# Attention weights and values: one fp32 product in place of three split products

## What is computed

```python
z = einsum('bhtd,bhsd->bhts', qb, kb) * scale
causal = s_idx < t_idx
log_beta = log_sigmoid(z)
log_skip_j = where(causal, log_sigmoid(-z), 0.0)
log_skip = cumsum(log_skip_j, axis=3, reverse=True) - log_skip_j
weights = where(causal, exp(log_beta + log_skip), 0.0)
outs.append(einsum('bhts,bhsd->bhtd', weights, vb))
```

## Time and profile before

| | |
|---|---|
| median of three runs | 1186.79 us |
| the profiled execution | 1186.26 us |
| its span, first to last instruction | 1184.4 us |
| PE (TensorE matmul) busy | 1171.7 us, 99% of the span |
| DVE (VectorE) busy | 783.7 us, 66% |
| ACT (ScalarE) busy | 419.6 us, 35% |
| POOL (GpSimd) busy | 148.8 us, 13% |
| mean granted TensorE clock | 0.997 |

### The profile page before, as it was taken

One profiled execution on the slowest core, in us unless ns is written; L12 is line 12 of the kernel. 1 busy time (PEld: TensorE's weight loads), 2 busy tenths in 40 slices (PEclk: granted clock), 3 DMA queues, 4 the chain that ended last, 5 costly groups with the idle time before them and its releaser, 6 DMA issues. The chain is left out here.

```text
span 1184.4 us, 20326 instructions
## 1 busy us (share of the span) xinstructions
PE 1171.7 (99%) x7268; PEld 1078.3 (91%) x7268; DVE 783.7 (66%) x1576; ACT 419.6 (35%) x911; POOL 148.8 (13%) x344
## 2 busy tenths in 40 slices
PE   8999999999999999999999999999999999999998
PEld 7999999999999999887888989898999999999787
DVE  5657485766767675673544777778787878788521
ACT  4545353545445453552222222323232222222200
POOL 2322121213031311110003100000000000000000
PEclk8999999999999999999999999999999999999999
DMA  8220223223132301065632110314141421117431
GB/s 241 62 54 19 72 81 103 77 82 102 70 115 72 108 1 46 10 243 197 200 107 72 54 36 19 116 64 145 61 142 65 139 75 52 46 36 282 158 138 71
DMA packets 110657, 113.49 MB, mean 96 GB/s; under 512 B 6880, under 2 KB 86752, under 8 KB 110560
## 3 DMA queue, kind: packets, MB, share of 16 engines
q1 hardware_dynamic: 110560, 112.23, 29.6%
HBM read 79.70 MB, written 32.51 MB: 95 GB/s over the span
## 5 line engine op out<-in xcount | busy, mean ns | idle before, releaser
L28 PE MATMUL p_proj<-w_qkv_hi,ut_hi 128*128 128x384 f32 x512 | 176.1, 344 | 2.5 <-DVE ut_lo L792 2.5
L30 PE MATMUL p_proj<-w_qkv_hi,ut_lo 128*128 128x384 f32 x512 | 173.0, 338 | 0.0
L29 PE MATMUL p_proj<-w_qkv_lo,ut_hi 128*128 128x384 f32 x512 | 172.5, 337 | 0.0
L28 PE MATMUL p_proj<-w_ig_hi,next_hi 128*128 128x256 f32 x512 | 145.7, 284 | 0.0
L29 PE MATMUL p_proj<-w_ig_lo,next_hi 128*128 128x256 f32 x512 | 143.1, 280 | 0.0
L30 PE MATMUL p_proj<-w_ig_hi,next_lo 128*128 128x256 f32 x512 | 143.1, 280 | 0.0
L28 PE MATMUL p_proj<-next_hi,w_qf_hi 128*128 128x512 f32 x282 | 113.3, 402 | 0.0
L30 PE MATMUL p_proj<-next_hi,w_qf_lo 128*128 128x512 f32 x282 | 110.2, 391 | 0.0
L29 PE MATMUL p_proj<-next_lo,w_qf_hi 128*128 128x512 f32 x282 | 109.9, 390 | 0.0
L804 DVE TENSOR_TENSOR_SCAN a_skip<-a_skip,a_diagonal 128x129 f32<-128x129 f32 (+3 forms) x64 | 86.9, 1358 | 31.5 <-ACT a_beta L648 29.6
L28 PEld LDWEIGHTS p_proj<-w_qkv_hi,ut_hi 128*128 128x128 f32 x512 | 97.1, 190 | 3.9 <-DVE w_qkv_lo L772 2.4
(11 more groups left out here) (238 smaller groups left out, 2751.2 us busy)
## 6 DMA issues: line engine op xcount, KB each, us to landing
stage<-in_hg_w_in_dram SPq DMA_DIRECT2D x32, 512.0 KB, 4.6
stage<-in_sb_w_in_dram SPq DMA_DIRECT2D x29, 512.0 KB, 5.8
w_out_hi_scratch<-m_in SPq DMA_DIRECT2D x32, 256.0 KB, 2.1
w_out_lo_scratch<-m_in SPq DMA_DIRECT2D x32, 256.0 KB, 2.3
m_in<-mixed_scratch SPq DMA_DIRECT2D x12, 448.0 KB, 5.8
a_beta<-in_x_dram SPq DMA_DIRECT2D x8, 512.0 KB, 4.4
m_in<-in_sb_w_out_dram SPq DMA_DIRECT2D x16, 256.0 KB, 3.8
ut_hi<-w_out_hi_scratch SPq DMA_DIRECT2D x8, 512.0 KB, 8.5
```

The lines of the kernel that those rows point to most:

```text
L28: pe.matmul(out, w_hi, m_hi, start=start, stop=False, skip_group_check=True)
L29: pe.matmul(out, w_hi, m_lo, start=False, stop=False, skip_group_check=True)
L30: return pe.matmul(out, w_lo, m_hi, start=False, stop=stop, skip_group_check=True)
```

## The change

Values are kept in one fp32 tile `v`, written by one copy of VectorE. Weights are kept in one fp32 tile `wt`, written by ScalarE's copy, which now raises `wt_ready` itself. VectorE's `split_weights` is gone, and with it the semaphores `wt_hi_ready` and `v_hi_ready`. `outputs` makes one fp32 product per block. The tables, the projections, the scores and all of layer 1 are as before.

```diff
-        v_hi = [sb(f"v_hi{b}", [P, TILES, P], F32R) for b in range(2)]
-        v_lo = [sb(f"v_lo{b}", [P, TILES, P], F32R) for b in range(2)]
+        v = [sb(f"v{b}", [P, TILES, P]) for b in range(2)]
...
-        wt_hi = sb("wt_hi", [P, TILES, 2, P], F32R)
-        wt_lo = sb("wt_lo", [P, TILES, 2, P], F32R)
+        wt = sb("wt", [P, TILES, 2, P])
...
-                act.activation(wt_hi[:, blocks, j % 2, :],
-                               bank[:, 0:blocks.stop - blocks.start, :], ACT.Copy).then_inc(wt_hi_ready, 1)
+                act.activation(wt[:, blocks, j % 2, :],
+                               bank[:, 0:blocks.stop - blocks.start, :], ACT.Copy).then_inc(wt_ready, 1)
...
-            def split_weights(h, j, u, bank):
-
-                dve.wait_ge(wt_hi_ready, UNITS * h + ENDS[j] - Z_UNITS[j] + u + 1)
-                if not (known_first(h) and j < 2):
-                    dve.wait_ge(o_done, PAIRS * h + j // 2)
-                blocks = unit_blocks(j, u)
-                dve.tensor_tensor(wt_lo[:, blocks, j % 2, :], bank[:, 0:blocks.stop - blocks.start, :],
-                                  wt_hi[:, blocks, j % 2, :].bitcast(F32),
-                                  ALU.subtract).then_inc(wt_ready, 1)
...
-                        dve.tensor_copy(v_hi[nb][:, t, :], raw[t % 4][:, 2, :]).then_inc(v_hi_ready, 1)
-                        dve.wait_ge(v_hi_ready, NAT * n + t + 1)
-                        dve.tensor_tensor(v_lo[nb][:, t, :], raw[t % 4][:, 2, :], v_hi[nb][:, t, :].bitcast(F32),
-                                          ALU.subtract).then_inc(v_ready, 1)
+                        dve.tensor_copy(v[nb][:, t, :], raw[t % 4][:, 2, :]).then_inc(v_ready, 1)
...
-                    w_h = wt_hi[:, s, :, :] if s <= 2 * g else wt_hi[:, s, 1, :]
-                    w_l = wt_lo[:, s, :, :] if s <= 2 * g else wt_lo[:, s, 1, :]
-                    last = matmul_exact(pe, o, v_hi[b][:, s, :], v_lo[b][:, s, :], w_h, w_l,
-                                        s == 0, s == 2 * g + 1)
+                    last = pe.matmul(o, v[b][:, s, :], wt[:, s, :, :] if s <= 2 * g else wt[:, s, 1, :],
+                                     start=s == 0, stop=s == 2 * g + 1, skip_group_check=True)
```

More of the change, by code:

```diff
@@ L425, in build_attention @@
         raw_ready = sem("raw_ready")
-        v_hi_ready = sem("v_hi_ready")
         v_ready = sem("v_ready")
@@ L441, in build_attention @@
         weights_turned = sem("weights_turned")
-        wt_hi_ready = sem("wt_hi_ready")
         wt_ready = sem("wt_ready")
@@ L821, in attend @@
                         last_head_lo(half, tile)
[L822 to L825, removed]
             def last_head_lo(b, part):
```

## The result

The changed kernel takes 1192.17 us (median of five runs, 1191.01 to 1192.68) against 1187.15 us before (1186.08 to 1187.77, five runs). The ratio is 1.0042, with a 95% interval of 1.0031 to 1.0052: slower by 5.0 us, where 8.0 us was forecast. The profiled execution took 1192.68 us, the slowest of the five. TensorE's granted clock was 1.00, the 2.4 GHz level, from 17 us to the end of the products in both profiled executions, so their rows may be compared directly.

What follows compares the result with a forecast made beforehand. TensorE's streaming was taken to bound the kernel (99% busy): +10.5 us of streaming less 2.5 of stalls gives +8.0, from 1186.26 to 1194.3 us for the profiled execution, 1194.8 for the median; range 1190.5 to 1198.5.

Steps and rivals of the forecast that it cites:

- Two instructions, two passes: In outputs, one fp32 product is two instructions, each streaming its columns twice; likeliest case, 0.88 with its whole range.
- The price of 0.45 us: Cost of one 256-column fp32 product in outputs, 0.43 to 0.46 us, against 0.352 split; streaming +10.5 us in all.
- the cheap end: Low end of the likeliest case: 0.43 us a product and 4.2 us of stalls gone, +3.7, 1190.5 us; no own chance.
- The stalls: TensorE's waits at three places for the weights' lower part: 2.5 us given back, at least 1.2, at most 4.2.
- the first stall: TensorE's wait around 497.25 us, before outputs: 1.4 us, of which 0.9 comes back and 0.5 stays, for ScalarE's copy.
- the second: TensorE's wait before the outputs at 529.97 us, behind VectorE's scan and product: 1.15 us, all of it to go.
- third: TensorE's last wait for the lower part, after the product ending at 537.72 us: 0.45 us, all to go.
- What costs nothing: VectorE's lost work, ScalarE's copy and later `o_done` and `o_gated` add no time; layer 1 lasts as long as before.
- The bound of 3 us: If cover failed at the last eight groups of outputs (0.7 us): under 3 us, 1 us kept in the range.
- One pass: Rival: every fp32 instruction streams once, 0.235 us per 256-column product in outputs, 1167.3 us in all; chance 0.08.
- Three passes: Rival: an fp32 product's two instructions stream three times together, 0.35 us, level with split; chance 0.04, including level results.
- The level rival: Three passes in outputs: only 2.1 us of 128-column gain and 2.5 of stalls left, 1182.3 us; chance 0.04, including level results.

Runs made afterwards that it cites:

- The experiment that takes the waits alone: Changed kernel with F32R tiles and three products per block, all of upper parts, lower parts left out (doesn't compute the reference): 1184.82 us, ratio 0.999.
- The two kernels run side by side: "Streaming only" again, 1194.59 us (ratio 1.0068), and the same with the second VectorE operation on each value tile put back, 1193.07 us (ratio 1.0053).
- Streaming only: Changed kernel with VectorE's subtraction of the weights put back, into a tile that nothing reads, and raising `wt_ready`: 1194.1 us, ratio 1.0063.

## Why the prediction was right

The sign and the mechanism held: TensorE's stream sets the time, one fp32 product is two instructions that each take up about the time of twice their columns, and VectorE's relief is worth only the stalls. The size was 8.0 us where 5.0 was measured. The account of the 5.0 is: +8.0 of streaming, -1.3 at the other products of the attention, -2.5 of stalls, +0.8 in layer 1. Step by step:

- **Two instructions, two passes.** Right. The trace after has 320 instructions for 160 products, 0.216 us apart at 256 columns and 379 ns long (390 was forecast), and halving the width changes little. The decisive rows were the durations of the earlier trace rows; the steps of 0.11 us would have been the same either way. The reading of the earlier trace rows worked with a slightly smaller step than it names (0.06 us for 128 columns gives 191 and 176 ns, not 193 and 178), and 195 fits 64 columns all the same. What the runs can't tell apart is an instruction that makes two passes and one that streams once at half the rate: the time is the same. The rule of the Trainium skill that a true fp32 product makes four passes through the array ("FP8 and Floating Point Precision", "TensorE Precision Notes") agrees with this better than three would: 0.432 us is 3.7 times the 0.1173 us of one F32R instruction.
- **The price of 0.45 us.** This is the term that was mis-sized most. It is 0.432 us, near the cheap end of 0.43: 2.3 us less over 128 products. The rest of the 2.5 us is in the narrow products. I had put 256 columns streamed twice at the price of F32R's 512 columns, 0.22 to 0.23 us, and it is 0.216. Streaming grew by 8.0 us, not 10.5.
- **The stalls.** 2.5 us was forecast, and 2.5 went. By the ends the first stall fell from 1.4 to 0.5 us, which stay for ScalarE, as written, and the second (1.16) and third (0.46) went in full. The experiment that takes the waits alone gives 2.5 in the attention.
- **The products around the outputs.** The sum had no term for them, as it took each product's price to be its own. They took up 1.3 us less, most of it at the one product behind each group of outputs. That is the second largest part of the miss.
- **What costs nothing.** The cover held in layer 0: no new wait for `o_done` or `o_gated` reached TensorE. The bound of 3 us on it was not worked out rightly, since 0.7 us at each of eight groups is 5.6 us; only the reason given, that the tables of two heads run close, made it smaller. The claim failed in a place that I hadn't looked at. Layer 1 was to start 8 us later and last as long as before. In the profiles the attention ends 4.3 us later, and layer 1 lost 0.8 us to the pause of VectorE. I took the removal of instructions for free because no engine waits for an instruction that isn't there; the pause sits elsewhere in the new program.
- **The rivals.** One pass was refuted by the first trace after (a step of 0.216 and not 0.12). Three passes likewise (that would be 0.175). The cheap end, 1190.5, was nearest on streaming. It also took 4.2 us of stalls as gone, and 2.5 went. Two effects that no sum had, the -1.3 us around the outputs and the +0.8 us of the pause, nearly cancelled, and that is luck. The level rival adds up to 1182.2 us, not 1182.3; nothing hangs on it.

## What to carry to other kernels

On a kernel that TensorE bounds, count the passes: three split F32R products against four passes of one fp32 product. The fp32 one loses where the columns set the pace (256 columns: 0.432 against 0.352 us) and wins where the weight load does (128 columns: 0.221 against 0.284 us, or against 0.33 us where the split ones follow each other without a wider one ahead), so choose product by product and not for a whole stage. Done so here, on 24 products alone, it made the kernel 2.6 us faster where the whole stage made it 5.0 us slower. Price the product behind the changed one too: it came up to 0.05 us sooner here. Where two operations have the same distance of starts, look at their shortest durations before calling them equal: the load of weights can hide a second pass.

## What the runs showed of the hardware that was not expected

An fp32 instruction of 256 columns takes up 0.216 us; an F32R instruction of 512 columns takes up 0.229 us, and two of 256 columns 0.235 us. So for the same number of columns through the array fp32 costs less. By an estimate from these figures and the 2.4 GHz level, it is 1.01 periods of the clock for a column (each counted twice) against 1.07 to 1.10.

The product that follows a group of outputs comes sooner when the last output is fp32: a transpose 0.109 us after it and not 0.130, a 128-column product of split operands 0.06 and not 0.11. It is so in all eight profiles that have fp32 products at that place, and in none of the four that haven't.

VectorE pauses for 1.6 to 2.8 us with nothing waited for, and the place goes with its program and not with TensorE's: before `a_skip` in the attention in the six profiles whose kernel has a second operation on each value tile, before `g_k_left` in layer 1 in the six whose kernel hasn't. The two kernels run side by side show that; it cost TensorE 0.8 to 1.1 us in the second place and nothing in the first. The length alone isn't shown to decide it. "Streaming only" has 96 VectorE instructions more than the changed kernel and pauses before the same one. A second gap, of 1.0 to 1.3 us, stands before the same `g_scores` near the end of layer 1 in every profile, before and after. What the pauses are, the loading of instructions or something else, isn't shown.
